# Short convolution's decode columns in three operations, 31-tap convolution's input and decode products on GpSimd, its taps begun earlier, and the mixer's end reordered

## What is computed

```python
def decoder_layer(x, ...):
    h = x + 0.5 * rms_norm(swiglu(rms_norm(x, f1_pre), ...), f1_post)
    p_all = rms_norm(h, m_pre) @ w_in
    ya = conformer_conv(...)   # a = val * sigmoid(gate); 31 taps; layer norm; silu
    yb = gla_mixer(...)        # gated linear attention, chunks of 64
    yc = short_conv(...)       # z = cg * xv; y = bg * (3 taps of z)
    yd = fox_prompt / fox_decode(...)   # attention with a forget bias
    h = h + rms_norm(concatenate([ya, yb, yc, yd]) @ w_out, m_post)
    return h + 0.5 * rms_norm(swiglu(rms_norm(h, f2_pre), ...), f2_post)

def causal_depthwise(xpad, w):   # y[t] = sum over taps of xpad[t + tap] * w[tap]
```

## Time and profile before

| | |
|---|---|
| median of 3 runs | 1067.48 us (1067.37 to 1069.41) |
| profiled execution | 1067.81 us, span 1066.0 us |
| TensorE busy | 1052.3 us (99% of the span) |
| VectorE busy | 687.6 us (64%) |
| ScalarE busy | 571.5 us (54%) |
| GpSimd busy | 278.4 us (26%) |
| granted TensorE clock | 0.9 or more of full speed in every slice |

### The profile page before, as it was taken

The page is one execution under the profiler, slowest core; times in us unless marked ns, Lnnn a source line. Parts: engine busy times, 40 slices in busy tenths (PEclk is TensorE's granted clock), DMA queues, the critical chain, the costliest instruction groups (busy, mean ns, idle before and its releaser), DMA issues. The chain is left out here.

```text
span 1066.0 us, 24197 instructions
## 1 busy us (share of the span) xinstructions
PE 1052.3 (99%) x8978; PEld 1022.7 (96%) x8978; DVE 687.6 (64%) x1032; ACT 571.5 (54%) x970; POOL 278.4 (26%) x344
## 2 busy tenths in 40 slices
PE   8999999999999999999999999999999999999997
PEld 8999999998989999999999999999988999999997
DVE  5666644599977666654476666446999776666442
ACT  6544454576467644454464444546665765444542
POOL 4222220204505222220142222103054233222202
PEclk9999999999999999999999999999999999999999
DMA  7666577453735665556646656763536356665551
GB/s 277 216 180 186 175 223 235 127 160 92 226 100 182 199 192 179 180 168 184 185 135 199 179 177 186 234 200 118 174 102 213 109 176 216 179 188 175 174 182 49
DMA packets 62882, 187.42 MB, mean 176 GB/s; under 512 B 9162, under 2 KB 18514, under 8 KB 62674
## 3 DMA queue, kind: packets, MB, share of 16 engines
q1 hardware_dynamic: 62802, 186.31, 57.3%
HBM read 182.90 MB, written 3.38 MB: 175 GB/s over the span
## 5 line engine op out<-in xcount | busy, mean ns | idle before, releaser
L318 DVE TENSOR_TENSOR w_lo<-raw,w_hi 128x1024 fp32r<-128x1024 f32 (+1 forms) x316 | 412.3, 1310 | 321.7 <-ACT w_hi L308 321.6
L308 ACT ACTIVATE w_hi<-raw 128x1024 fp32r<-128x1024 f32 x336 | 344.9, 1032 | 238.5 <-PE ub L352 171.2
L350 PE MATMUL ub<-hg_hi,w_hi 128*128 128x264 f32 x976 | 281.2, 288 | 1.2 <-issue 1.2
L351 PE MATMUL ub<-hg_lo,w_hi 128*128 128x264 f32 x976 | 276.6, 283 | 0.0
L352 PE MATMUL ub<-hg_hi,w_lo 128*128 128x264 f32 x976 | 276.3, 283 | 0.0
L350 PE MATMUL ub<-act_hi,w_hi 128*128 128x264 f32 x704 | 200.5, 285 | 0.0
L352 PE MATMUL ub<-act_hi,w_lo 128*128 128x264 f32 x704 | 200.0, 284 | 0.0
L351 PE MATMUL ub<-act_lo,w_hi 128*128 128x264 f32 x704 | 199.1, 283 | 0.0
L350 PE MATMUL quad<-hg_hi,w_hi 128*128 128x264 f32 x696 | 198.6, 285 | 0.0
L351 PE MATMUL quad<-hg_lo,w_hi 128*128 128x264 f32 x696 | 197.2, 283 | 0.0
L352 PE MATMUL quad<-hg_hi,w_lo 128*128 128x264 f32 x696 | 197.1, 283 | 0.0
(11 more groups left out here) (259 smaller groups left out, 1285.3 us busy)
## 6 DMA issues: line engine op xcount, KB each, us to landing
raw<-in_w_gu SPq DMA_DIRECT2D x176, 512.0 KB, 4.0
raw<-in_w_dn SPq DMA_DIRECT2D x64, 512.0 KB, 3.9
raw<-in_w_in SPq DMA_DIRECT2D x44, 512.0 KB, 3.7
raw<-in_w_dn SPq DMA_DIRECT2D x32, 384.0 KB, 3.5
raw<-in_w_out SPq DMA_DIRECT2D x16, 512.0 KB, 3.7
pages<-in_cache_k SPq DMA_DIRECT2D x32, 128.0 KB, 3.4
pages<-in_cache_v SPq DMA_DIRECT2D x32, 128.0 KB, 3.1
con<-in_con SPq DMA_DIRECT2D x1, 1192.0 KB
```

The source lines that it names most:

```text
L308: eng.activation(w_hi[:, slot, 0:w], raw[:, slot, 0:w], ACT.Copy).then_inc(*sig("hi_ready", reps))
L318: eng.tensor_tensor(w_lo[:, slot, 0:w], raw[:, slot, 0:w], w_hi[:, slot, 0:w].bitcast(F32), ALU.subtract)\
L350: eng.matmul(out, a_hi, x_hi[:, k0 + k, :], start=(first and k == 0), stop=False)
L351: eng.matmul(out, a_hi, x_lo[:, k0 + k, :], start=False, stop=False)
```

## The change

- The 31-tap convolution's input `a_pad` and the new decode column `a_dec` are made by GpSimd (`conv_inputs`), after `clear_pads` and ahead of the rests of unit 14. They wait for unit 9's evacuation (`proj=10`).
- Its 31-tap decode products are GpSimd's too (`conv_products`), between the rests of units 19 and 20. The reduction stays on VectorE.
- Taps 0 to 2 stand in slot 11 now, and their sum in SBUF, in the place of the result (`ymix`, printed as yg); tap 3 reads it there, waits for the last mask and goes on in PSUM. The table `TAPS` begins at slot 11 and ends with one tap in slot 19.
- The short convolution's decode columns of both groups are three operations (`short_decode`): the new column, 48 products, one reduction. They stand in slot 22.
- `d_all` moves from slot 23, behind the gate, to the end of slot 22. Head 3's transposes go to `mb[2]`, and wait for `d_tmp`, the last reader of that bank (`d_dt=1`), not for the copy of head 0.

```diff
 POOLED = tuple(range(14, 24))
-TAPS = {12: (0, 4), 13: (4, 10), 15: (10, 16), 16: (16, 22), 17: (22, 26), 18: (26, 28), 19: (28, 31)}
+TAPS = {11: (0, 3), 12: (3, 7), 13: (7, 11), 15: (11, 17), 16: (17, 23), 17: (23, 27), 18: (27, 30), 19: (30, 31)}
+EARLY_TAPS = 3
 
...
         z_dec = sb("z_dec", [P, 2, TD, TAPS_C])
+        c_prod = sb("c_prod", [P, 2, TD, TAPS_C])
         st = sb("st", [P, TD, DV])
...
         fox_bank = (mb[0], mb[1], ub[2], mb[2])
-        turned_bank = (mb[0], mb[1], ub[3], mb[0])
+        turned_bank = (mb[0], mb[1], ub[3], mb[2])
         taps_sum = ub[3]
...
                 if part == 3:
-                    sp.wait_ge(*at(l, "c_z1", 3))
-                    sp.wait_ge(*at(l, "c_z", 3))
+                    sp.wait_ge(*at(l, "c_z1", 2))
+                    sp.wait_ge(*at(l, "c_zd", 1))
                     sp.dma_start(outs["pc"][bass.ds(l, 1)].rearrange("a p c t -> p (a c) t"), z_pad[:, :, TP:TP + 2]).then_inc(*sig("stored", n=16))
...
                 if h == 3:
-                    after(l, d_pt=1)
+                    after(l, d_dt=1)
                 for i in range(3):
...
                         k = 2 * t + c
-                        y, x, w = taps_sum[:, c * TP:(c + 1) * TP], a_pad[:, c, t:t + TP], par[:, PAR["acw"] + c * TAPS_A + t:PAR["acw"] + c * TAPS_A + t + 1]
+                        x, w = a_pad[:, c, t:t + TP], par[:, PAR["acw"] + c * TAPS_A + t:PAR["acw"] + c * TAPS_A + t + 1]
+                        early, late = ymix[:, YA + c, 0:TP], taps_sum[:, c * TP:(c + 1) * TP]
                         if t == 0:
-                            after(l, b_msk=7)
-                            dve.tensor_scalar(y, x, w, par[:, PAR["acb"] + c:PAR["acb"] + c + 1], ALU.mult, ALU.add).then_inc(*sig("a_tap"))
+                            after(l, a_in=1)
+                            dve.tensor_scalar(early, x, w, par[:, PAR["acb"] + c:PAR["acb"] + c + 1], ALU.mult, ALU.add).then_inc(*sig("a_tap"))
                         else:
                             after(l, a_tap=k - 1)
-                            out = ymix[:, YA + c, 0:TP] if t == TAPS_A - 1 else y
-                            dve.scalar_tensor_tensor(out, x, w, y, ALU.mult, ALU.add).then_inc(*sig("a_tap"))
+                            if t == EARLY_TAPS:
+                                after(l, b_msk=7)
+                            out = early if t < EARLY_TAPS or t == TAPS_A - 1 else late
+                            dve.scalar_tensor_tensor(out, x, w, early if t <= EARLY_TAPS else late, ALU.mult, ALU.add).then_inc(*sig("a_tap"))
 
...
                     dve.tensor_scalar(cf[:, 0:TP], cf[:, 0:TP], -8.0, None, ALU.mult).then_inc(*sig("d_cf"))
-                if n == 11:
-
-                    after(l, a_sg=1, a_z=1, proj=10)
-                    dve.tensor_tensor(a_pad[:, :, TAPS_A - 1:], proj[:, AV:AV + 2, 0:TP], proj[:, AG:AG + 2, 0:TP], ALU.mult).then_inc(*sig("a_in"))
-                    after(l, past=PAST)
-                    dve.tensor_tensor(a_dec[:, :, :, TAPS_A - 1], proj[:, AV:AV + 2, TP:NT], proj[:, AG:AG + 2, TP:NT], ALU.mult)\
-                       .then_inc(*sig("a_in"))
                 if n == 13:
...
                     dve.tensor_reduce(dstat[:, 1:2], sd[:, :], AX.X, ALU.max, negate=True).then_inc(*sig("d_dmx"))
-                    after(l, a_in=2)
-                    for c in range(2):
-                        dve.tensor_tensor(a_prod[:, c, :, :], a_dec[:, c, :, :],
-                                          par[:, PAR["acw"] + c * TAPS_A:PAR["acw"] + (c + 1) * TAPS_A].unsqueeze(1).to_broadcast([P, TD, TAPS_A]),
-                                          ALU.mult).then_inc(*sig("a_dp"))
                     after(l, a_dp=2)
...
                     short_conv(l, 1)
+                    short_decode(l)
                     rest_mixed(l, YB)
-                if n == 23:
-                    short_gate(l, 0)
                     after(l, d_dpv=2)
...
                                       const("own", 2 * H).unsqueeze(2).to_broadcast([P, 2 * H, DV]), ALU.mult).then_inc(*sig("d_dall"))
+                if n == 23:
+                    short_gate(l, 0)
                 if n == 24:
...
                 dve.tensor_tensor(z[:, 2:], proj[:, CC + 2 * c, 0:TP], proj[:, CX + 2 * c, 0:TP], ALU.mult).then_inc(*sig(name))
-                dve.tensor_tensor(z_dec[:, c, :, 2], proj[:, CC + 2 * c, TP:NT], proj[:, CX + 2 * c, TP:NT], ALU.mult).then_inc(*sig(name))
-                after(l, **{name: 3})
+                after(l, **{name: 2})
                 done = ("c_t", "c_t1")[c]
                 for t in range(TAPS_C):
-                    for y_t, z_t1 in ((y[:, 0:TP], z[:, t:t + TP]), (y[:, TP:NT], z_dec[:, c, :, t])):
-                        if t == 0:
-                            dve.tensor_scalar(y_t, z_t1, w[t], None, ALU.mult).then_inc(*sig(done))
-                        else:
-                            dve.scalar_tensor_tensor(y_t, z_t1, w[t], y_t, ALU.mult, ALU.add).then_inc(*sig(done))
-                    after(l, **{done: 2 * t + 2})
+                    if t == 0:
+                        dve.tensor_scalar(y[:, 0:TP], z[:, t:t + TP], w[t], None, ALU.mult).then_inc(*sig(done))
+                    else:
+                        dve.scalar_tensor_tensor(y[:, 0:TP], z[:, t:t + TP], w[t], y[:, 0:TP], ALU.mult, ALU.add).then_inc(*sig(done))
+                    after(l, **{done: t + 1})
+
+            def short_decode(l):
+
+                dve.tensor_tensor(z_dec[:, :, :, 2], proj[:, CC:CC + 3:2, TP:NT], proj[:, CX:CX + 3:2, TP:NT], ALU.mult).then_inc(*sig("c_zd"))
+                after(l, c_zd=1)
+                dve.tensor_tensor(c_prod[:, :, :, :], z_dec[:, :, :, :],
+                                  par[:, PAR["ccw"]:PAR["ccw"] + 2 * TAPS_C].rearrange("p (c t) -> p c t", c=2).unsqueeze(2).to_broadcast([P, 2, TD, TAPS_C]),
+                                  ALU.mult).then_inc(*sig("c_zp"))
+                after(l, c_zp=1)
+                dve.tensor_reduce(ymix[:, YC:YC + 2, TP:NT], c_prod[:, :, :, :], AX.X, ALU.add).then_inc(*sig("c_zr"))
+                after(l, c_zr=1)
 
...
 
+            def conv_inputs(l):
+
+                after(l, a_sg=1, a_z=1, proj=10)
+                pool.tensor_tensor(a_pad[:, :, TAPS_A - 1:], proj[:, AV:AV + 2, 0:TP], proj[:, AG:AG + 2, 0:TP], ALU.mult).then_inc(*sig("a_in"))
+                after(l, past=PAST)
+                pool.tensor_tensor(a_dec[:, :, :, TAPS_A - 1], proj[:, AV:AV + 2, TP:NT], proj[:, AG:AG + 2, TP:NT], ALU.mult)\
+                    .then_inc(*sig("a_in"))
+
+            def conv_products(l):
+
+                after(l, a_in=2, b_o=1)
+                for c in range(2):
+                    pool.tensor_tensor(a_prod[:, c, :, :], a_dec[:, c, :, :],
+                                       par[:, PAR["acw"] + c * TAPS_A:PAR["acw"] + (c + 1) * TAPS_A].unsqueeze(1).to_broadcast([P, TD, TAPS_A]),
+                                       ALU.mult).then_inc(*sig("a_dp"))
+
             for t, name in ((qd[:, :], started), (pm[:, :], zeroed), (lfp[:, :], S["stored"]), (lfn[:, :], S["stored"])):
...
                 clear_pads(l)
+                conv_inputs(l)
                 for n in POOLED:
+                    if n == 20:
+                        conv_products(l)
                     rest_halves(pool, l, n)
```

More of the change, by code:

```diff
@@ L1563 @@
     "a_tap": 62, "rest_half": 20, "b_kvm": 2, "b_S": 3, "b_kvd": 8, "b_prod": 8, "d_ct": 3, "a_dr": 1, "a_db": 1,
-    "d_ds": 2, "d_dmx": 1, "d_sm": 4, "d_dri": 1, "d_dp": 2, "d_mx": 2, "b_t": 2, "b_y": 1, "d_ri": 4, "d_pn": 8, "ym_ready": 8, "a_cen": 2, "a_nrm": 1, "c_z1": 3, "c_t1": 6, "c_y1": 1, "d_dt": 1, "d_dy": 1,
+    "d_ds": 2, "d_dmx": 1, "d_sm": 4, "d_dri": 1, "d_dp": 2, "d_mx": 2, "b_t": 2, "b_y": 1, "d_ri": 4, "d_pn": 8, "ym_ready": 8, "a_cen": 2, "a_nrm": 1, "c_z1": 2, "c_t1": 3, "c_zd": 1, "c_zp": 1, "c_zr": 1, "c_y1": 1, "d_dt": 1, "d_dy": 1,
     "act_ready": 44, "act_lo": 44, "y_acc": 24, "h_acc": 27, "a_z": 1, "b_qe": 1,
     "a_in": 2, "b_vx": 16, "b_sde": 8, "b_gs": 1, "b_sd": 1, "a_dp": 2,
-    "d_pm": 2, "c_z": 3, "c_t": 6, "c_y": 1
+    "d_pm": 2, "c_z": 2, "c_t": 3, "c_y": 1
 }
```

## The result

| | before | after |
|---|---|---|
| median of 5 runs | 1067.59 us (1067.37 to 1069.41) | 1072.77 us (1072.54 to 1073.09) |
| profiled execution | 1067.81, span 1066.0 | 1072.77, span 1071.0 |
| TensorE busy | 1052.3 us | 1052.9 us |
| VectorE, GpSimd busy | 687.6, 278.4 us | 692.8, 285.4 us |

The account below looks back on a forecast made before the run. TensorE was busy 1052.3 of 1066.0 us, so only waits of its own queue counted. Per layer 3.08 lost minus 1.36 gained is 1.72, 3.4 for two: 1070.9 against a median of 1067.48; eight-in-ten range 1066.3 to 1073.0.

Parts of the forecast that it names:

- Structure and sign: Whole change: front's loss outweighs the end's gain, so slower by 3.4 us; chance of slower 0.49.
- The end: Mixer's end: waits before head 3's transposes (0.84) and before `decode_gather` (0.52) go, a gain of 1.36 per layer.
- the end gives nothing: Rival at the mixer's end: `d_tmp` late or new bank waits, 1.36 per layer missing, 1073.6; 0.10 with the dearer product.
- The short convolution: Its eight small VectorE operations become three, saving about 0.9 us that TensorE's full queue hides: cost 0, gain 0.
- the decode products on GpSimd: Two 31-tap operations ahead of unit 20's rest fit into GpSimd's 3.95 us idle time: nothing.
- The front: Slots 10 and 11: input products on GpSimd and early taps delay unit 11's evacuation, a loss of 3.08 per layer.
- No queue for the ports: Rival in slot 11: GpSimd's product doesn't hold up VectorE, 2.05 per layer gained, 1063.4; chance 0.17.
- half of the queue: Rival in slots 10 and 11: turns fall more kindly, evacuation 11 late by about 1.2, time 1067.2; chance 0.13.
- a dearer product: Rival: `a_pad` on GpSimd takes 2.5 us instead of 1.27, time 1073.3; 0.10 together with the end giving nothing.
- The gain open at `decode_scores`: TensorE's start there moves earlier with unit 11's evacuation, by at most 1.2 us.
- The open price: Whether L1225's SBUF-to-SBUF `tensor_scalar` takes turns with GpSimd: 3.08 late if so (taken, 0.38), 2.35 if not (0.22).
- The order of the turns: Slot 10: GpSimd's half 1 goes ahead of VectorE's weight rest, which ends 249.54; level 6 starts at 250.7.

Follow-up runs that it names:

- e1: Changed kernel with input products back on VectorE in slot 11 and taps from slot 12 as before; 1066.31 us, ratio 0.9972.
- e2: Kernel before with only the input products on GpSimd and the early taps in slot 11; 1074.23 us, ratio 1.0052.
- e3: Changed kernel with the taps back where they were, from slot 12, input products still on GpSimd; 1067.17 us, ratio 0.9989.
- e7: e4 with taps dealt out anew, eight tap operations in slot 13 in place of 12; 1062.61 us, ratio 0.9941.
- e8: Changed kernel with GpSimd's input products moved behind unit 14's rest, taps dealt out as in e7; 1064.23 us, ratio 0.9956.
- e10: Changed kernel with the scaling of the fox gates (L1230) moved from slot 10 to slot 13; 1072.85 us, ratio 1.0039.
- e4: e1 with the input products on VectorE in slot 12, ahead of mask 6; 1068.15 us, ratio 0.999.
- e9: Changed kernel with two tap operations in slot 11 in place of six, the others dealt to later slots; 1069.68 us, ratio 1.0008.
- e12: Changed kernel with two tiny VectorE fills at the very start of the program; 1072.32 us, ratio 1.0032.
- e11: e8 with one tiny VectorE fill per layer in slot 10; 1062.41 us, ratio 0.9941.

## Why the prediction was right, and where it was short

**Structure and sign: right.** Predicted 1070.9 in 1066.3 to 1073.0, measured 1072.77. That is near the upper end, and above the 1069.3 to 1071.6 that the forecast gave itself without its rivals. (The chances as listed add up to 0.17 faster, 0.35 same and 0.48 slower, not 0.18, 0.33 and 0.49.)

**The end, -1.36 per layer: right.** Measured -1.46 and -1.45, of which 0.84 are the step at the transposes of head 3 and 0.52 and 0.50 that at the gather; the same within 0.1 in the eleven experiments that kept the end. The rival in which the end gives nothing falls. The short convolution and the decode products on GpSimd were put at nothing: in e1, which keeps both, no other stretch of layer 0 moved.

**The front, +3.08 per layer: right in size.** Measured 1.63 + 1.56 = 3.19 and 1.65 + 1.53 = 3.18, and e2 alone gives 3.18 in both layers. The chain is the one that was put down: evacuation 11, `v_diag`, `decode_scores`. Seen in before's time, with 0.27 for the faster start-up of this execution, evacuation 11 came at 254.07 (predicted 253.97) and `decode_scores` at 265.52 (about 265.4). *No queue for the ports* falls with keys 6 at 1.46; *half of the queue* falls with e2, and *a dearer product* with `a_pad` at 1.28. The gain open at `decode_scores` was put at 1.2 at most; where `v_diag` came early (e3, e7, e8) it was 1.33 to 1.36.

**The open price: settled as taken.** A `tensor_scalar` from SBUF to SBUF takes its turn: 1.38 beside a half of GpSimd, 0.28 to 0.30 alone. The Trainium skill (SBUF — State Buffer, "SBUF: two separate sides") has two-port modes in the lock; these rows agree.

**The order of the turns: partly wrong.** I had GpSimd's second half ahead of VectorE's weight rest, so the rest at 2.3 us and level 6 at 250.7. The rest got in first (247.07, 1.21 long), level 6 started at 249.42 and waited 1.6 instead of 2.6. In return both early `tensor_scalar` taps stood behind a half (2.67), where I had let one through. GpSimd's halves fall in the same stretch whoever stands behind which, and e10 shows the same: a turn that is avoided is taken by the next operation. Two errors of about 1.1 us cancelled, so the term was right partly by luck.

**What the sum lacked: 1.8 us, in two places of layer 1.** 5.25 is lost by the traces, 3.4 was summed. 1.57 is the order at the second feed-forward's start, a loss by position in the program that no row of the mixer could tell. 0.35 is at L651 (L649 before): ScalarE's normalisation stands behind a weight that lands late. One issue of SyncE ahead of that place took 1.51 us in the change and 0.43 in the kernel before, but it took 1.52 in e3 and 1.85 in e7, which lose nothing there, so the long issue alone is not the cause. The piece was 0.35 and 0.73 in two traces of the same kernel, and between 0 and 1.25 over all; its cause stays open.

**A step of my own experiments that failed.** In e4 and e9 I read the wait of `decode_scores` off the load of VectorE's later slots. It is fixed 11.0 us behind the start of `v_diag`, as long as unit 13's evacuation is no later.

## What to carry to other kernels

Before work goes to GpSimd, look at what VectorE has beside it: here the operations with an operand in PSUM ran on, while two-input products, scans and a `tensor_scalar` that live in SBUF alone waited a whole instruction, and what counts is who stands behind them. The same two products cost 3.2 us a layer, with the taps pulled forward beside GpSimd's rests, and gave 1.3 two halves of a rest later, or on VectorE behind the one evacuation that was urgent. Ask which single event the next engine hangs on (here unit 11's evacuation), keep everything else behind it, then look for what is next late: here unit 13's, by four tap operations too many.

## What the runs showed of the hardware

- **VectorE and GpSimd take turns by whole instructions on SBUF.** 512 elements of a two-input product: 0.68 alone, 1.46 beside GpSimd; a `tensor_scalar` of 256: 0.28 and 1.38; a scan of 256: 0.68 and 1.76; GpSimd's 16-element product 0.23 alone, 0.68 in turns. Operations with an operand in PSUM kept their 0.42 to 0.44 (evacuation) and 0.72 to 0.75 (mask) beside GpSimd's rests.
- **An instruction's position in the program can cost a microsecond.** VectorE's L1111 started 0.13 us late with 1349 records ahead of its `hg_lo`, and not with 1351, 1363 or 1365. By itself that is nothing, but it let GpSimd in first at the shared memory, and the pattern of operations behind it then lost 1.57 us (0.64 in e12). A fill of 0.06 us or two removed it or moved it. Why is not shown. Kernels compared at 0.1% should be compared by trace as well.
- **A wait can cost TensorE its clock behind it.** In e4 a wait of 2.3 us at L629 was followed by 3.4 us at a granted clock of 0.5 (1.2 GHz), which cost 1.6 us more. Behind the waits of 1.6 and 1.5 us in the mixer of the change it stayed at full speed.
- **The start-up varies** by up to 1.6 us at 81 us into the traces, though these kernels' instructions are the same up to there but for e12's fills; the five slowest of fourteen had the clock at 0.5 for 3.4 us. The kernel before alone spread from 1067.4 to 1070.7 over the runs.
- **e7 and e11 are the fastest here,** 1062.61 and 1062.41 beside 1068.93 and 1069.01 for the kernel before; behind the first 20.5 us the view of waits shows none of TensorE in either.
